# A transformer trunk on one core: an expert's overflow product moved between two base products, and three weight chunks loaded as 112 + 8 + 8 rows

## What is computed

```python
def moe_swiglu(h, w_router, w_gate, w_up, w_down):
    t = h.reshape(B * S, D)                       # 256 tokens, D = 1024
    logits = jnp.dot(t, w_router)
    top_val, top_idx = lax.top_k(logits, TOP_K)   # 2 of 8 experts for each token
    gates = jax.nn.softmax(top_val, axis=-1)
    ...
    for e in range(N_EXPERTS):                    # D_FF_EXPERT = 3584
        out = out + combine[:, e:e + 1] * swiglu(t, w_gate[e], w_up[e], w_down[e])
```

## Time and profile before

| What | Value |
|---|---|
| Median of 3 runs | 1144.1 us (1142.36 to 1144.64) |
| The profiled execution | 1142.71 us, of which the span is 1140.9 us |
| PE busy | 1123.9 us (99%) |
| DVE, ACT, POOL busy | 312.3, 136.8, 17.2 us |
| Granted TensorE clock, mean | 0.998 |
| Read from memory | 400.61 MB |

### The profile page before, as it was taken

How to read it: one execution, slowest core, us unless ns; L and a number is a source line. 1 busy time by engine, 2 the same in 40 slices (tenths; PEclk the granted TensorE clock), 3 DMA queues, 4 the chain that set the end, 5 groups by cost and what they waited for, 6 DMA issues and landing times.

```text
span 1140.9 us, 14902 instructions
## 1 busy us (share of the span) xinstructions
PE 1123.9 (99%) x6247; PEld 497.1 (44%) x6248; DVE 312.3 (27%) x561; ACT 136.8 (12%) x293; POOL 17.2 (2%) x58
## 2 busy tenths in 40 slices
PE   9999999999999999999999999999999989999996
PEld 7645566764553334343333334333333423333332
DVE  3556865666541111110201011020101101110102
ACT  1452011110131100000101000010100001110001
POOL 2300000000000000000000000000000000000000
PEclk9999999999999999999999999999999999999999
DMA  7535333447298999999999999999999999999994
GB/s 298 221 119 213 148 147 113 190 177 302 106 432 359 401 402 425 433 430 428 428 431 432 430 427 431 429 429 430 431 429 429 429 432 427 428 431 427 429 425 196
DMA packets 19702, 402.92 MB, mean 353 GB/s; under 512 B 3360, under 2 KB 3360, under 8 KB 4256
## 3 DMA queue, kind: packets, MB, share of 16 engines
q1 hardware_dynamic: 19616, 401.67, 83.5%
HBM read 400.61 MB, written 1.05 MB: 352 GB/s over the span
## 4 chain that ended last, share of the span: by engine, by line
PE 91%; DMA 7%; DVE 1%; ACT 0%; issue 0%; SPq 0%; DVEq 0%; ACTq 0%
PE bank L1789 33%; PE bank L1919 14%; PE bank L1521 12%; PE bank L1760 9%; PE bank L1556 6%; DMA ring<-moe_w_up 4%; DMA ring<-moe_w_down 3%; PE bank L1950 2%; PE bank L1468 2%; PE bank L1851 2%; PE bank L1412 2%; PE bank L1720 1%; PE bank L1743 1%; PE bank L1702 1%; DMA ring<-attn_w_qkv 1%; PE bank L1379 1%
## 5 line engine op out<-in xcount | busy, mean ns | idle before, releaser
L1789 PE MATMUL bank<-ring,arena 128*64 128x448 f32 x2048 | 393.3, 542 | 3.1 <-DMA ring<-moe_w_up 2.3
L1789 PEld LDWEIGHTS bank<-ring,arena 128*64 128x64 f32 x2048 | 145.0, 137 | 249.1 <-issue 244.1
L1919 PE MATMUL bank<-ring,arena 128*64 128x512 f32 x896 | 198.7, 595 | 1.2 <-DMA ring<-moe_w_down 1.0
L1521 PE MATMUL bank<-ring 128*128 128x384 f32 (+1 forms) x448 | 134.4, 459 | 0.0
L1919 PEld LDWEIGHTS bank<-ring,arena 128*64 128x64 f32 x896 | 62.1, 137 | 123.1 <-issue 120.0
L1248 DVE TENSOR_TENSOR arena<-bank,arena 128x448 f32<-128x448 f32 x32 | 20.0, 624 | 331.3 <-PE bank L1789 331.3
L1521 PEld LDWEIGHTS bank<-ring 128*128 128x128 f32 x448 | 84.3, 190 | 45.8 <-issue 0.5
L1760 PE MATMUL bank<-ring,arena 128*32 128x448 f32 x1024 | 99.7, 541 | 0.0
L1760 PEld LDWEIGHTS bank<-ring,arena 128*32 128x32 f32 x1024 | 31.5, 110 | 64.4 <-issue 64.4
L918 DVE TENSOR_TENSOR ring<-ring 128x1536 f32<-128x1536 f32 (+2 forms) x35 | 53.2, 1540 | 10.3 <-PE bank L1455 9.3
L762 ACT ACTIVATE arena<-bank 128x448 f32<-128x448 f32 x32 | 17.4, 543 | 283.6 <-PE bank L1789 283.4
(11 more groups left out here) (217 smaller groups left out, 683.8 us busy)
## 6 DMA issues: line engine op xcount, KB each, us to landing
ring<-moe_w_gate SPq DMA_DIRECT2D x31, 3584.0 KB, 21.9
ring<-moe_w_up SPq DMA_DIRECT2D x31, 3584.0 KB, 26.1
ring<-moe_w_down SPq DMA_DIRECT2D x29, 3584.0 KB, 25.1
ring<-ffn_w_gate SPq DMA_DIRECT2D x3, 3072.0 KB, 10.1
ring<-ffn_w_up SPq DMA_DIRECT2D x3, 3072.0 KB, 10.1
ring<-ffn_w_down SPq DMA_DIRECT2D x3, 3072.0 KB, 10.0
ring<-moe_w_down SPq DMA_DIRECT2D x3, 2048.0 KB, 31.0
ring<-moe_w_down SPq DMA_DIRECT2D x3, 1536.0 KB, 34.2
```

The lines of the kernel that those rows point to most:

```text
L1521: last = mm(ffn_bank(m, i), b[lhs][:, k, :], b[rhs][:, k, :], start=k == 0, stop=k == 3)
L1789: last = mm(bank[2 * (j % 2) + up][64 * h:64 * h + 64, 0:FJ], xg[:, k, side:side + BASE], w[:, k, h, :], start=k == 0, stop=k == KD - 1)
L1919: last = mm(bank[2][64 * h:64 * h + 64, :], hg[:, i0 + i, half * BASE:half * BASE + BASE], w[:, i, h * BANK:h * BANK + BANK], start=d == 0 ...
```

## The change

Two things. The variable `apart` holds for the first two pairs of the first expert instead of the first alone, so in pair j = 1 of `it` = 0 the overflow gate product runs straight behind the base gate product. The flag is still read once, in pair 0. And chunk 3 (the up chunk of pair 1) of `it` = 2, 4 and 6 is loaded by three transfers instead of one: rows 0 to 111, rows 112 to 119, rows 120 to 127. The first counts on `full[slot]` as before, the other two on a semaphore of their own, for which PE waits besides before the base up product.

```diff
+ROW_GROUP = 8
...
+        last_rows = [sem(f"last_rows{n}") for n in range(3)]
...
+        def in_rows(it, c):
+
+            return {(2, 3): 0, (4, 3): 1, (6, 3): 2}.get((it, c)) if isinstance(it, int) else None
...
+                elif in_rows(it, c) is not None:
+                    at = P - 2 * ROW_GROUP
+                    sp.dma_start(ring[s][0:at, :], w[0:at, :]).then_inc(full[s], 16)
+                    for r in range(at, P, ROW_GROUP):
+                        sp.dma_start(ring[s][r:r + ROW_GROUP, :], w[r:r + ROW_GROUP, :]
+                                     ).then_inc(last_rows[in_rows(it, c)], 16)
...
-                apart = not looped and it == 0 and j == 0
+                apart = not looped and it == 0 and j < 2
...
+                    if in_rows(it, c) is not None:
+                        pe.wait_ge(last_rows[in_rows(it, c)], 32)
...
-                    if apart and not up:
+                    if apart and c == 0:
                         pe.wait_ge(flags_ready, 1)
                         ext = flag(it + 1)
```

## The result

| What | Before | After |
|---|---|---|
| Median | 1144.37 us (6 runs) | 1205.26 us (6 runs, 1200.95 to 1206.98) |
| Ratio | | 1.0537, 95% interval 1.0523 to 1.0551 |
| Span of the profiled execution | 1140.9 us | 1203.4 us |
| Granted TensorE clock, mean | 0.998 | 0.977 |
| Last weight rows landed, about | 1128 us | 1189 us |

The kernel became 60.9 us slower. One of the six runs before took 1976.86 us; the ratio leaves it out, and without it the median before is 1144.1 us. The prediction (1142.8 us, range 1140.4 to 1157.0) was wrong, and its range too.

What follows compares the result with a forecast made beforehand. The weight stream, ended by the late half of the DMA engines, was taken to bound the kernel. Part one's +0.3 us and part two's load shift made -1.3 us together, from 1144.1 to 1142.8 us; range 1140.4 to 1157.

Steps and rivals of the forecast that it cites:

- What bounds the kernel: Whole kernel: the weight stream, a little slower than PE, sets the end from 928 us on.
- Part one, +0.3 us: First expert's pair 1, overflow gate behind base gate: two more form switches on PE cost +0.3 us (0 to +0.3).
- More transfers as such, nothing: Three cut chunks: extra issues and split transfers cost nothing, or 0.2 us.
- 112 rows give each 7: Cut chunks' large piece: each of 16 engines carries 7 rows, at 1.07 us a row.
- Eight rows on eight engines: Cut chunks' small pieces: each reaches only eight engines; the same eight give 9 rows against 7, 3.2 us over three chunks.
- Cases A and B: Which engines carry the eights: A, early half, -1.3 us, chance 0.46; B, late half or mixture, +3.5 us, chance 0.14.
- Case C: Eights' neighbouring rows share a way into on-chip memory: 4.3 us a row, full price +17 us, staggered +8; chance 0.24.

Runs made afterwards that it cites:

- e1: Kernel before with the overflow gate reordering of the first expert's second pair alone, all chunks as one transfer: 1143.22 against 1143.19 us, ratio 1.0002.
- e4: Kernel before with the three chunks each in three transfers cut by columns (6272, 448, 448), all 128 rows in each: 1144.62 us, ratio 1.0007.
- e5: Kernel before with the three chunks each as 112 + 16 rows, no transfer of eight: 1193.51 against 1143.05 us, ratio 1.0431.
- e7: Kernel before with the three chunks each as rows 32 to 127 and four transfers of eight neighbouring rows: 1204.11 us, ratio 1.0532.
- e12: Kernel before with cuts by rows: expert 2 even and odd 64, expert 4 four times every fourth row, expert 6 120 + 8: 1159.84 us, one run.
- e10: Kernel before with 96 rows and four eights per cut chunk, eights written to neighbouring rows, read from every fourth: 1206.00 us, ratio 1.0544.
- e11: Kernel before with 96 rows and four eights per cut chunk, eights written to every fourth row, read from neighbouring rows: 1192.41 us, ratio 1.0420.
- e15: Kernel before; expert 2: every second row within each half; expert 4: written even/odd, read in halves; expert 6: written in halves, read even/odd: 1170.77 us, one run.
- e8: Kernel before with the three chunks each as rows 32 to 127 and four eights of every fourth row: 1192.23 us, ratio 1.0420.
- e16: Kernel before; expert 2: rows 32-95, 0-31, 96-127; expert 4: 8-127, 0-7; expert 6: 32-95 by every second, 0-31, 96-127: 1187.53 us, one run.
- e2: Kernel before with the chunk cuts alone, three chunks as 112 + 8 + 8 rows, no gate reordering: 1207.37 us, ratio 1.0554.
- e6: Kernel before; expert 2: eight transfers of 16 rows eight apart; expert 4: eight of 16 neighbouring rows; expert 6: two of 64: 1187.88 us, one run.
- e17: Kernel before, two chunks cut as 64 even rows, 32 odd, four eights; eights in lower half for expert 2, upper for expert 4: 1166.96 us, ratio 1.0206.

## Why the prediction was wrong

**What bounds the kernel**: right. The stream sets the end; the median rose by 60.9 us, the last landing by 61.0.

**Part one, +0.3 us**: right, by every sign: 18.61 us for the pair, chunk 8 issued 6.3 us earlier in the kernel after (355.81 us), chunk 0 of the next expert not earlier (399.95), ratio 1.0002 in all for e1.

**More transfers as such, nothing**: right (e4: six more transfers and the wait, ratio 1.0007 with 1 inside the interval).

**"112 rows give each 7" at 1.07 us a row**: this is the step that failed. The count of rows was right, the time of a row was not: 2.0 us. The 1.07 us came from the earlier trace rows, where every transfer has 128 rows, and I carried it over to another set of rows without a bound. 7 rows x 1 us too long on every engine is at least 7 us a chunk, and e5 shows 13 to 20 us. The rest is a second thing that the prediction put at nothing: the engines that are still at the chunk ahead, or already at the next, go at half rate too (25.6 to 46.1 us for a cut chunk in the kernel after, where a whole one takes 8.5). I had asked for the eights "what if rows get in each other's way" and never asked it for the 112.

**Eight rows on eight engines**: right, by two counts. The semaphore of a chunk's two eights shows 16 counts at landings, eight for each. The main queue has 19664 packets in the kernel after and 19616 in the one before, 48 more for six eights; 48 more as well for three 16-row pieces (e5), and 96 more for twelve eights (e7). So it looks as if a piece costs one packet more for each engine that carries it, eight for an eight; e12's 71 more fit too, with 15 for its 120 rows.

**Cases A and B**: something shifts between engines, as the tail shows, and it looks most like the mixture that case B allowed for: most of the early half loaded, and two late engines with it, which end 6 and 8 us behind the others (0.13 of the share in the tail). Which engines these are isn't shown. With the half rate present nothing of A's -1.3 us can show, and no run had eights without slow rows; whether a shift could ever pay wasn't tried in a clean form.

**Case C** came nearest, in the wrong size and place. It priced rows that share a way into the on-chip memory: up to 4.3 us a row for the eights (3.8 us measured at 548 us), +17 us in all, and it gave the case 0.24. But it looked at the six eights alone, which e5 puts at 10 to 14 of the 61 us. The other 50 us are there without any eight, with 112 + 16 rows. That it is one mechanism in the small and the large piece is likely, since the written side decides in both (e10, e11, e15), but not shown. It also said where to look: the dips, and waits from expert 4 or earlier (the first is at 694 us, in expert 3).

What decides is where the rows of one transfer are written. Sorted by e5 to e8, e12, e15 and e16:

| Rows of a transfer | Rate |
|---|---|
| all 128; every second (64) or fourth (32) of all; 32 to 95 in one piece | full, 416 to 459 GB/s |
| 0 to 63; every second of 0 to 63; every eighth of all (16); 0 to 31 | half, 203 to 244 GB/s |
| 0 to 111; 32 to 127; 0 to 119; 8 to 127 | half, 210 to 232 GB/s |
| 16 neighbouring rows, eight such pieces in a row; every second of 32 to 95 (32) | half, 221 and 237 GB/s |

The Trainium skill, SBUF — State Buffer, section "Door 1: The DMA port swizzle", gives a map of 16 ports: four neighbouring partitions share one, the pattern repeats after 32 partitions, and partitions from 64 up use the other eight. By it the first line of the table are just the sets that fall evenly on all 16 ports, and each set of the second line reaches only eight: these runs agree, with half the rate for half the ports, and rows 32 to 95 were foretold by it. The lower two lines don't follow from the number of ports: the sets of the third reach all 16, every second row of 32 to 95 reaches all 16 evenly, 16 neighbouring rows reach four, and all of them went at half rate. There the measurement decides. The same skill, DMA: Bandwidth & Descriptors, section "The descriptor swizzle", says that in a 128-partition transfer each engine writes one port of its own; no row names an engine, but that would fit whole chunks at full rate (430 GB/s), and a cut that breaks the pairing would fit the losses of the lower two lines. This is argued, not shown. It would also have been the question to ask in step one: the map was cited against the eights, and nobody asked what the 112 rows do to that pairing.

**What stays open.** The lower two lines. 112 or 120 rows reach all 16 ports, only unevenly (by the map 8 rows on most and 4 on the others), which for 112 would by count make 8 row times of 7, a seventh more, and they take twice as long. That engines on each other's ports hold one another up, even when the counts are nearly even, is argued and not shown. That a later chunk costs more because the engines are further apart there fits every alike cut of the kernel after, e2, e5, e6 and e7's first chunk (0.46 to 0.56 of the stretch lost), but no run changed the distance alone. Nor is it shown why far eights go at 2.2 us.

## What to carry to other kernels

A rate measured with full 128-row transfers holds for those; before a load is cut by rows, ask which partitions each piece writes, and cut by columns with all 128 rows where it can be done (here at no cost). If it must be rows, take every second or fourth of all 128 for every piece of the chunk (0.0 to 0.2 us lost in e12 and e15, one run each), and not a block such as 0 to 63 or 0 to 111. A DMA share of 1.00 says that engines are occupied, not that they move much: read GB/s beside it.

## What the runs showed of the hardware

- A transfer written to 120, 112, 96 or 64 neighbouring rows (0 to 119, 0 to 111, 32 to 127, 0 to 63) goes at 212 to 232 GB/s where 128 rows go at 430, with all engines shown as busy: 2.0 to 2.2 instead of 1.07 us for a row of 28,672 bytes. How the rows lie in the memory that is read made no difference in either test (e10 and e11, e15).
- The exception 32 to 95 (416 to 444 GB/s) has as many neighbouring rows as 0 to 63 (212). Every second row of 32 to 95 is slow again (237).
- The slow rate also holds for others: in e17 the windows from 756 to 770 us stay at 186 to 229 GB/s until the last eights have landed at 772 us, while by the counts on its semaphore the first engine was through with the next, whole chunk at 762.3 us. In e16 no row of any chunk that began between 961 and 990 us took under 1.78 us.
- Two of 16 engines can end 6 and 8 us after all others (1187.0 and 1189.0 against 1181.0 us) and hold up everything: the share in the tail is 0.13.
